# A cache-rope scratch in DRAM, laid out for 128 partitions of 4096 bytes instead of 64 of 8192

## The reference, cut to what matters

```
s = (jnp.einsum('bqhc,bkc->bhqk', q_lat, c_kv) + jnp.einsum('bqhr,bkr->bhqk', q_rope, k_rope)) * ATTN_SCALE
def step(carry, pages):                    # one page of 128 keys for each sequence
    m, l, acc = carry
    ck, kr = cache_ckv[pages], cache_krope[pages]
    s = mla_scores(q_lat, q_rope, ck, kr)
    m_new = jnp.maximum(m, jnp.max(s, axis=-1)); alpha = jnp.exp(m - m_new)
    p = jnp.exp(s - m_new[..., None])
    l = l * alpha + jnp.sum(p, axis=-1)
    acc = acc * alpha[..., None] + jnp.einsum('bhqk,bkc->bhqc', p, ck)
    return (m_new, l, acc), None
```

## Time and profile before

| | us |
|---|---|
| median of 3 executions | 2001.77 |
| lowest and highest | 1987.11, 2001.91 |
| the profiled execution: its own time | 1993.43 |
| its span | 1991.6 |

### The profile page before, as it was taken

How to read it: one execution, slowest core, us unless ns; L and a number is a source line. 1 busy time by engine, 2 the same in 40 slices (tenths; PEclk the granted TensorE clock), 3 DMA queues, 4 the chain that set the end, 5 groups by cost and what they waited for, 6 DMA issues and landing times. The chain is left out here.

```text
span 1991.6 us, 28826 instructions
## 1 busy us (share of the span) xinstructions
PE 1807.6 (91%) x11390; PEld 1235.3 (62%) x11390; DVE 733.5 (37%) x1659; ACT 451.5 (23%) x998; POOL 309.4 (16%) x428
## 2 busy tenths in 40 slices
PE   7989999999979999989999997998598888898884
PEld 5678888888846665756665664565455555565551
DVE  3343334444323433344554554465222311111116
ACT  3122211111122323233343433222010100101113
POOL 1024211111100000001111112253311211111100
PEclk9999999999989999999999998999698999998997
DMA  7112225555620000028999984535599999999986
GB/s 217 47 66 76 76 69 206 207 211 211 226 83 1 1 1 1 1 64 237 293 300 273 309 288 180 197 134 204 191 419 420 419 418 416 412 406 393 414 346 263
DMA packets 105004, 432.93 MB, mean 217 GB/s; under 512 B 24192, under 2 KB 29792, under 8 KB 74112
## 3 DMA queue, kind: packets, MB, share of 16 engines
q1 hardware_dynamic: 84608, 330.01, 44.1%
q0 software_dynamic: 20160, 101.24, 15.4%
q10 hardware_dynamic: 128, 0.20, 0.0%
HBM read 388.17 MB, written 63.66 MB: 227 GB/s over the span
## 5 line engine op out<-in xcount | busy, mean ns | idle before, releaser
L914 PE MATMUL psum<-arena 128*128 128x256 f32 x1792 | 392.9, 379 | 2.5 <-DVE arena L2079 2.0
L914 PEld LDWEIGHTS psum<-arena 128*128 128x128 f32 x1792 | 337.0, 189 | 56.6 <-issue 5.4
L1383 PE MATMUL psum<-arena 128*64 128x256 f32 (+1 forms) x2048 | 283.7, 411 | 64.8 <-DMA arena<-in_w_up_dram 64.6
L1383 PEld LDWEIGHTS psum<-arena 128*64 128x64 f32 (+1 forms) x2048 | 204.7, 155 | 134.0 <-issue 81.3
L2426 DVE TENSOR_TENSOR arena<-arena,psum 128x256 f32<-128x256 f32 x36 | 15.2, 421 | 319.1 <-ACT arena L1683 319.1
L1402 PE MATMUL psum<-arena 128*64 128x512 f32 (+1 forms) x512 | 131.4, 595 | 1.2 <-DMA arena<-in_w_down_dram 1.2
L1141 PEld LDWEIGHTS psum<-arena 128*128 128x128 f32 x1024 | 112.7, 141 | 29.5 <-issue 27.9
L1141 PE MATMUL psum<-arena 128*128 128x128 f32 x1024 | 126.5, 276 | 0.0
L1271 PE MATMUL psum<-arena 128*128 128x512 f32 x256 | 113.2, 599 | 1.3 <-ACT arena L1618 1.3
L1583 ACT COPY arena<-psum 128x512 f32<-128x512 f32 x128 | 71.7, 587 | 177.8 <-PE psum L1141 177.8
L1897 POOL DMA_INDIRECT y_rows<-arena x36 | 40.6, 1129 | 410.7 <-DVE arena L2435 392.9
(11 more groups left out here) (328 smaller groups left out, 2189.7 us busy)
## 6 DMA issues: line engine op xcount, KB each, us to landing
arena<-in_w_gate_dram SPq DMA_DIRECT2D x64, 1024.0 KB, 14.1
arena<-in_w_up_dram SPq DMA_DIRECT2D x64, 1024.0 KB
arena<-in_w_down_dram SPq DMA_DIRECT2D x64, 1024.0 KB, 21.9
arena<-in_w_in_dram SPq DMA_DIRECT2D x8, 2048.0 KB, 11.2
z_act<-arena SPq DMA_DIRECT2D x64, 256.0 KB
rope_turned<-arena SPq DMA_DIRECT2D x32, 512.0 KB
arena<-rope_turned SPq DMA_DIRECT2D x64, 256.0 KB
arena<-z_act SPq DMA_DIRECT2D x8, 2048.0 KB, 9.6
```

The source lines that it names most:

```text
L914: last = mm(out[:, 0:256], x[:, k, :], w[:, k, :], start=(k == 0), stop=(k == 3))
L1383: last = mm(bank(2 + u)[rows, DE * x:DE * x + DE], xg_t[u][:, k, rows], w_e[slot][x][:, k, :], start=(k == 0), stop=(k == KD - 1))
```

## The change

The DRAM scratch holds a chunk in the order in which TensorE will want it: row h*64 + c*32 + f has the rope number c*32 + f for the keys of half h (j = 0, 1 for h = 0, and j = 2, 3 for h = 1), 1024 numbers in all. The 32-partition blocks and the two halves have to be put in place by the stores, so one store of 512 KB becomes 8 stores (`N_ST`) of 64 KB: each takes 32 partitions, and 2 runs of 1024 bytes from each. The load of a chunk becomes one DMA of 128 partitions of 4096 bytes in place of two of 32 partitions with four runs of 2048 bytes. A home is now a tile of its own of 128 partitions by 4096 bytes; there are still four, in the same space. In the scores, j = 0 and 1 read the lower 64 partitions and j = 2 and 3 the upper ones, in every chunk. The counts that are waited for follow. VectorE's turning and GpSimd's gathers are not changed.

```
+        N_ST = 8
-        kr_t2 = [take(PG * P, o) for _ in range(2)]
+        kr_t2 = [take(PG * DR, o) for _ in range(4)]
         def rope_home(n):
-            return kr_t2[n % 4 // 2][DR * (n % 2):DR * (n % 2) + DR, :]
+            return kr_t2[n % 4]
             def rope_store(n):
                 sp.wait_ge(rk_t, n + 1)
-                sp.dma_start(rope_t[P * n:P * n + P, :], kr_b[n % 2].rearrange("p c m -> p (c m)")).then_inc(rk_mv[n % 2], 16)
+                keys = rope_t[P * n:P * n + P, :].rearrange("(h c f) (a m) -> a h f c m", h=2, c=2, a=4)
+                for a in range(4):
+                    for h in range(2):
+                        sp.dma_start(keys[a, h], kr_b[n % 2][32 * a:32 * a + 32, :, 256 * h:256 * h + 256]).then_inc(rk_mv[n % 2], 16)
             def rope_load(n):
                 if n >= 4:
                     sp.wait_ge(c_s, n - 3)
-                sp.wait_ge(rk_mv[n % 2], 16 * PRE + 32 * (n // 2))
-                keys = rope_t[P * n:P * n + P, :].rearrange("(a f) (c m) -> c f a m", a=4, c=2)
-                for c in range(2):
-                    sp.dma_start(rope_home(n)[32 * c:32 * c + 32, :].rearrange("f (a m) -> f a m", a=4),
-                                 keys[c]).then_inc(rk_mv[n % 2], 16)
+                sp.wait_ge(rk_mv[n % 2], 16 * N_ST * PRE + 16 * (n // 2))
+                sp.dma_start(rope_home(n), rope_t[P * n:P * n + P, :]).then_inc(rk_mv[n % 2], 16)
             def score(n, q, loads):
-                half = slice(DR * (q % 2), DR * (q % 2) + DR)
-                rope = rope_home(q).rearrange("p (a r k) -> p r a k", a=4, r=PG)
+                rope = rope_home(q).rearrange("p (a r k) -> p r a k", a=4, r=PG // 2)
-                pe.wait_ge(rk_mv[q % 2], 16 * PRE + 32 * loads)
+                pe.wait_ge(rk_mv[q % 2], 16 * N_ST * PRE + 16 * loads)
                 for c in range(3):
                     for j in range(4):
+                        half, first = slice(DR * (j // 2), DR * (j // 2) + DR), 4 * (j % 2)
                         last = mm(bank(5)[RS * j:RS * j + RS, :], q_now[:, c, :] if c < 2 else qr_now[half, :],
-                                  ck_t[:, c, j, :] if c < 2 else rope[:, 4 * j:4 * j + 4], start=(c == 0), stop=(c == 2))
+                                  ck_t[:, c, j, :] if c < 2 else rope[half, first:first + 4], start=(c == 0), stop=(c == 2))
             for u in range(2):
-                pool.wait_ge(rk_mv[u], 16 * PRE)
+                pool.wait_ge(rk_mv[u], 16 * N_ST * PRE)
             def turn_rope(n):
-                    dve.wait_ge(rk_mv[n % 2], 16 * (n // 2))
+                    dve.wait_ge(rk_mv[n % 2], 16 * N_ST * (n // 2))
```

## The result

The change made the kernel a little slower: 2001.98 us is the median of 20 executions, where before has 1994.83 over 20, a ratio of 1.004 (1.0029 to 1.0052). The forecast was a gain of 2.9 us; measured is a loss of 7 to 8 (by the medians and by the ratio). The profiled execution took 1999.65 us, 6.2 more than that of before. 2001.98 us lies in the stated range (1981 to 2012), but that is no merit of the sum: the range is wide because of the level, and the step had the wrong sign. The level leaned on a median of 2001.77 over three executions of before, where twenty give 1994.83.

What follows compares the result with a forecast made beforehand. TensorE was taken as the bound in four of five parts, waiting for rope loads in the cache attention. -6.7 + 0 + 2 + 1.8 = -2.9 us took 1993.43 to 1990.5; forecast 1997, nearer to the median, range 1981 to 2012.

Steps and rivals of the forecast that it cites:

- What bounds the kernel, and the load: Cache attention: TensorE waits for rope rows; a chunk's load takes 1.41 us instead of 2.49, so 6.7 us come back.
- what is late next is nothing: Cache attention: with the rope waits gone, TensorE's own 8.73 us a chunk is the bound.
- more to gain: Rival, cache attention: slower executions may lose their extra 8.3 us in the same wait, giving 1991 us; chance 0.10.
- The scores: Cache attention: score matmuls reading lower and upper partitions side by side cost 0, low bound -4 us.
- one bank for two halves: Rival, scores: products of both halves can't write one bank at a time, +28 us, 2025; chance 0.08.
- The issue on SP: Projection: 8 stores at 0.456 us each, 3.65 us a chunk; the 16 issues fit in SP's slack.
- (a) The block's end: Projection: next block's 2 MB load slips, z stores queue behind it; 0 to 8 us over four blocks, taken as +2.
- (b) The projection's end: Projection's end: 16 issues take 7.3 us and 64 KB land in 2.2 us, so TensorE resumes later, +1.8 us.
- (c) w_uv: After the projection: this 1 MB load is issued at 556 and not 549.64, costing nothing, some 5 us to spare.
- the waits of this product line for VectorE behind the block ends: Projection: sign that the prediction is wrong, TensorE's products waiting for VectorE after block ends; no size given.
- stalls in the projection: Rival: issues of 0.79 us delay z stores, 10 to 25 us, at 2019; decides from 10 us; chance 0.10.

Runs made afterwards that it cites:

- e7: Kernel before with each rope load issued as one DMA to the same 64 partitions, rows of 8192 bytes; 1987.02 us in its one execution.
- e2: Changed kernel with the old single store of 512 KB a chunk, so rope numbers come to wrong places; 0.9977 of before, 1988.95 us.
- e8: Changed homes and score groups with the old single store, each chunk loaded by four DMAs of 32 partitions; 0.9973 of before, 1987.79 us.
- e13: Kernel before with the rope loads of chunks 4 to 31 cut from runs of 2048 bytes to 64; 0.9981 of before.
- e3: Changed kernel with the next block's 2 MB weight load issued ahead of the rope stores of a block's last pair; 1.0099 of before.
- e5: Changed kernel with the next block's 2 MB weight load issued by ScalarE on its own queue at a block's start; 1.0048 of before.
- e6: Changed kernel with FIRST_ROPE = 22 instead of 24, so turning and storing come two slots earlier; 0.9941 of before, 1979.03 us.
- e1: Kernel before with each rope store cut into 8 pieces of 64 KB, written to the old places, old loads kept; 1.0145 of before.
- e9: Kernel before with FIRST_ROPE = 22 and nothing else changed; 0.9950 of before, 1982.0 us.
- e15: Kernel before, unchanged, run once more for its profile; 1990.25 us.
- e16: Kernel before with FIRST_ROPE = 22, run once more for its profile; 1991.0 us.
- e10: Changed kernel with FIRST_ROPE = 21 instead of 24, so turning and storing come three slots earlier; 0.9992 of before.
- e11: Changed layout with 4 stores of 128 KB a chunk and FIRST_ROPE = 22; 0.9954 of before, 1982.4 us.
- e12: One store of 512 KB and four loads of 32 partitions a chunk, with FIRST_ROPE = 22; 0.9949 of before, 1981.8 us.

## Why the prediction was wrong, step by step

*What bounds the kernel, and the load.* Right in the profiled execution: -6.7 forecast, -6.8 measured, a load at 1.28 us for the 1.41 summed, "what is late next is nothing". I missed the gather's 1.2 us, and only the spare time under the period was affected. The Trainium skill (SBUF — State Buffer, Door 1: The DMA port swizzle), which gives 32 or 64 partitions 8 of 16 ports and some 218 GB/s, agrees with 211 GB/s for 32 partitions; for its equality of 64 and 32 partitions e7's 266 is no support, though that figure is a share of engine time beside a gather and no transfer alone. What failed is the use of one execution's wait as every execution's: by their ratios e2, e8 and e13 put the usual gain at 0.2 to 0.3%, some 4 or 5 us, with e13's interval down to nothing. The rival "more to gain" had it the wrong way round.

*The scores.* Right, 0: 34.8 us for 35.4. The rival of one bank for two halves is out, and with it the rule of the Trainium skill (TensorEngine Tiling (Array Packing), Gotcha 1: PSUM Pressure) that different row tiles can't access one PSUM bank at the same time, as far as it would slow two row tiles that write different rows of a bank.

*The issue on SP.* Right at the end, where 16 issues were summed at 7.3 us and took 7.65. Around the block ends they took more, 8.1 to 10.8 us (0.51 to 0.67 each): a fixed price of 0.456 was too low just where it mattered. SP's slack was enough all the same: in the first block the z stores were issued at 307.73 and 309.38, before at 308.03 and 309.76, and SP still waited for ScalarE ahead of 40 z stores within 290 to 570 us.

*(a) The block's end* is the first step that failed, in its size. SP and VectorE in the changed kernel:

```profile
296.41 9.03 SPq L681 DMA_DIRECT2D rope_turned<-arena  x16
305.48 0.43 SPq L690 DMA_DIRECT2D arena<-in_w_in_dram  x1
...
307.73 1.98 SPq L702 DMA_DIRECT2D z_act<-arena  x2
309.75 9.87 SPq L681 DMA_DIRECT2D rope_turned<-arena  x16
...
318.56 0.42 DVE L2098 TENSOR_TENSOR arena<-psum,arena 128x256 f32<-128x256 f32 x1 [8.44 <-DMA z_act<-arena]
```

The load slipped by 7.7 us and not 6.3, as the 16 issues took 9.0; the second z store landed at 318.5 where I had summed 317. Another 16 small stores, which the sum left out, were issued right behind the z stores. The overrun was put between 0 and 2 us a block and taken as 0.5: four times 0.5 is 2, and it was 7.5, at the top of the range of 0 to 8. The waits were 0.3 to 2.3 us, 5.1 together. The rest is 1.7 for the slower clock and some 0.3 us at each of the four breaks, since 224 instructions in one run take 48.72 us and in two pieces 21.03 + 27.95; against these stand 0.4 us by which the first block began earlier (296.06 for 296.44). A sum that ends within its own error of the deadline should have been priced at the middle of its range, 1 us at each of four ends; even so the forecast would have stayed a gain, of 0.9 us. What e3 and e5 add is that this wasn't the load's place alone: load, small stores and z stores shared a moment, and in each of the three orders one was late. In e6's order none was.

*(b) The projection's end* failed too, by 2.3 us: +1.8 summed, +4.1 measured. The issues were right but for 0.35 us; from the end of the last one to TensorE's start it took 4.2 us, where I had put the 2.2 of a lone 64 KB. The landing of these stores (us, of the changed kernel's 256) is this:

```profile
DMA to landing us min/median/max: 1.7/2.8/8.2
```

and GpSimd and the exchange at the stage's end come behind it; how the 4.2 us part between them isn't shown.

*(c) w_uv*, +0: right. It was issued at 563.89 and no product waited for it.

*The sum:* -6.7 + 0 + 7.5 + 4.1 in place of -6.7 + 0 + 2 + 1.8 is +4.9 for these steps in the profiles; in usual executions the gain is smaller and the block ends are dearer, +7 to +8. One of the prediction's own signs of being wrong came true, the waits of this product line for VectorE behind the block ends. *The rivals:* stalls in the projection was the right one in kind. Its price for an issue was not met (0.44 us in the median, not 0.79), but its line for deciding was: 16 issues and 2 z stores were to take 10 us, and took 11.0 at the first block's end. Its loss of 10 to 25 us didn't come, since SP was never full. What was shared and late was the landing behind SP's queue, so I tied the rival to the wrong resource. In e1, at 0.595, it came nearly as described.

## What to carry to other kernels

Cutting one DMA into eight cost, here, where the queue was shared, not where the bytes were: ask which later DMA has a deadline, sum its landing behind all that is now ahead, and price each place where the sum touches the deadline. Put the cut on the side where its issuing engine idles: here the loads, with SP waiting (e8), and not the stores. And before paying for a wait seen in one profile, look whether a second profile has it; the wait that every profile with FIRST_ROPE = 24 had, 9 us or more for the last store at a stage's end, was worth twice as much and took one constant.

## What I had not expected of the hardware

A DMA issue on SP took 0.30 us at the least for 64 KB in the changed layout, and 0.555 for the same bytes to the old places (medians 0.439 and 0.595), with equal partitions, runs and sizes. Nor is an issue's price fixed within a kernel: 16 of the changed kernel's took from 7.65 to 10.8 us. What sets it isn't shown.

The old loads slowed the gather beside them. A gather took 6.02 to 6.85 us of the engines in the five profiles with these loads (before, e1, e9, e15, e16; over 940 to 1060 us, worked out as for e15), 5.51 to 5.67 in the eight profiles with one load to 128 partitions (the changed kernel, e2 to e6, e10, e11), and 5.60 with hardly a load at all. In four pieces of 32 partitions (e8, e12) it was 6.02 and 5.78, and beside e7's load 6.77. The 5.60 is from these rows:

```profile
q0 software_dynamic: 1971, 28.62, 63.7%
q1 hardware_dynamic: 4032, 0.23, 2.3%
```

These are e13's queues within 940 to 1060 us. So a wide load cost the gather nothing that can be seen, and the narrow one up to half as much again as its own 2.4 us.
